# A two-block model on one core: keys, queries and attention of the sparse layer, rearranged

## What is computed

```python
# shared_kv, after the third FFN of the second block's first layer
kv = (u @ w_kv).reshape(b, s, 3, 2, N_KV_HEADS, HEAD_DIM)      # 3 branches, 2 key-value heads of 64
k_cmp = rms_norm(compress(kv[:, :, 0, 0], 0), kv_k_gain[0])    # 31 blocks of 32 tokens, stride 16
v_cmp = compress(kv[:, :, 0, 1], 1)                            # silu(flat @ phi_w1) @ phi_w2
k_slc = rope(rms_norm(kv[:, :, 1, 0], kv_k_gain[1]))           # and k_win in the same way
# nsa_mixer, after the next FFN: 16 query heads, 8 to a key-value head
q = rms_norm((u @ w_qg)[..., :1024].reshape(b, s, 16, 64), q_gain)
gates = sigmoid((u @ w_qg)[..., 1024:])                        # 48 columns
o = gates[0] * softmax(q @ k_cmp) @ v_cmp \
  + gates[1] * softmax(rope(q) @ k_slc) @ v_slc \
  + gates[2] * softmax(rope(q) @ k_win) @ v_win                # causal, no more than 512 keys
return o @ w_o
```

## Time and profile before

| | |
|---|---|
| median of 3 runs | 3986.0 us (3985.46 to 3986.86) |
| profiled execution, its own time | 3986.36 us |
| its span | 3984.6 us |
| TensorE busy, share of the span | 3708.1 us, 93% |
| VectorE busy | 1862.0 us, 47% |
| ScalarE busy | 1375.4 us, 35% |
| mean granted clock of TensorE | 0.955 |

### The profile page before, as it was taken

How to read it: one execution, slowest core, us unless ns; L and a number is a source line. 1 busy time by engine, 2 the same in 40 slices (tenths; PEclk the granted TensorE clock), 3 DMA queues, 4 the chain that set the end, 5 groups by cost and what they waited for, 6 DMA issues and landing times.

```text
span 3984.6 us, 49773 instructions
## 1 busy us (share of the span) xinstructions
PE 3708.1 (93%) x18908; PEld 2895.2 (73%) x18908; DVE 1862.0 (47%) x4004; ACT 1375.4 (35%) x2448; POOL 107.3 (3%) x183
## 2 busy tenths in 40 slices
PE   8879999989998999999999899999799997779999
PEld 3458966778887888777777678886688865557887
DVE  4656635566574333555445543331333327464333
ACT  1142212432233222555555542222222226463222
POOL 1100001011111000000000000000000000000000
PEclk9979999989999999999999999999699988999999
DMA  6500016336652222111111122321222210002222
GB/s 247 190 1 1 1 58 228 115 129 234 220 192 98 87 104 85 64 48 64 48 64 64 43 77 90 116 74 69 81 95 102 88 67 1 22 21 85 85 106 74
DMA packets 47289, 362.72 MB, mean 91 GB/s; under 512 B 5233, under 2 KB 5617, under 8 KB 28145
## 3 DMA queue, kind: packets, MB, share of 16 engines
q1 hardware_dynamic: 23616, 272.47, 18.7%
q0 software_dynamic: 23472, 87.50, 6.3%
HBM read 357.86 MB, written 2.10 MB: 90 GB/s over the span
## 4 chain that ended last, share of the span: by engine, by line
PE 81%; DVE 8%; issue 6%; ACT 2%; DVEq 1%; PEld 1%; DMA 0%; ACTq 0%; PEldq 0%; POOL 0%; SPq 0%; POOLq 0%
PE bank L792 19%; PE bank L798 19%; PE bank L797 19%; PE bank L755 6%; PE bank L1535 5%; PE bank L734 2%; PE bank L773 1%; PE bank L1869 1%; PE bank L1886 1%; PE bank L1857 1%; PE bank L708 1%; PE bank L722 1%; PE bank L1845 1%; DVE work_sb L2339 1%; DVE w_lo_sb L1154 1%
## 5 line engine op out<-in xcount | busy, mean ns | idle before, releaser
L792 PE MATMUL bank<-x_hi_sb,w_hi_sb 128*128 128x512 f32 x2592 | 1042.7, 402 | 62.5 <-DVE w_lo_sb L1154 15.5
L797 PE MATMUL bank<-x_lo_sb,w_hi_sb 128*128 128x512 f32 x2592 | 1019.6, 393 | 0.0
L798 PE MATMUL bank<-x_hi_sb,w_lo_sb 128*128 128x512 f32 x2592 | 1019.6, 393 | 0.0
L792 PEld LDWEIGHTS bank<-x_hi_sb,w_hi_sb 128*128 128x128 f32 x2592 | 493.1, 190 | 201.4 <-issue 77.5
L977 ACT ACTIVATE w_hi_sb<-slab_sb 128x1024 fp32r<-128x1024 f32 (+2 forms) x508 | 459.6, 930 | 403.2 <-PE bank L792 225.8
L1154 DVE TENSOR_TENSOR w_lo_sb<-slab_sb,w_hi_sb 128x1024 fp32r<-128x1024 f32 (+2 forms) x508 | 524.5, 1066 | 132.7 <-ACT w_hi_sb L977 116.2
L798 PEld LDWEIGHTS bank<-x_hi_sb,w_lo_sb 128*128 128x128 f32 x2592 | 493.0, 190 | 106.3
L797 PEld LDWEIGHTS bank<-x_lo_sb,w_hi_sb 128*128 128x128 f32 x2592 | 494.1, 191 | 96.3
L1305 DVE TENSOR_TENSOR hid_sb<-silu_gate_sb,bank 128x512 f32<-128x512 f32 x110 | 75.6, 688 | 624.2 <-PE bank L798 624.2
L792 PE MATMUL bank<-hid_hi_sb,w_hi_sb 128*128 128x512 f32 x880 | 343.3, 390 | 0.0
L798 PE MATMUL bank<-hid_hi_sb,w_lo_sb 128*128 128x512 f32 x880 | 342.8, 390 | 0.0
(11 more groups left out here) (336 smaller groups left out, 4095.2 us busy)
## 6 DMA issues: line engine op xcount, KB each, us to landing
slab_sb<-weights SPq DMA_DIRECT2D x81, 2048.0 KB, 7.7
slab_sb<-weights SPq DMA_DIRECT2D x44, 1536.0 KB, 6.4
keep_sb<-ada POOLq DMA_DIRECT2D x104, 512.0 KB, 4.8
slab_sb<-weights SPq DMA_DIRECT2D x20, 1280.0 KB, 5.9
work_sb<-ada POOLq DMA_DIRECT2D x49, 512.0 KB, 5.6
tables_sb<-ada POOLq DMA_DIRECT2D x7, 512.0 KB, 6.8
h_sb<-x SPq DMA_DIRECT2D x4, 512.0 KB, 7.4
out<-h_sb SPq DMA_DIRECT2D x8, 256.0 KB, 2.1
```

What stands on the lines that cost most here:

```text
L792: mm = pe.matmul(e.A.bank[s][:, :], w_hi[p][:, w], hi, start=first, stop=False)
L797: pe.matmul(e.A.bank[s][:, :], w_hi[p][:, w], lo, start=False, stop=False)
L798: return pe.matmul(e.A.bank[s][:, :], w_lo[p][:, w], hi, start=False, stop=last)
```

## The change

1. The weights of keys, compressed parts, values and all queries go the three-pass way. The key stage's order is: the 4 key tiles (an opening), the 2 compressed tiles, head sums, values, spread, compression of the keys, swap, compression of the values. The stages "kv" and "compress" are one.
2. The two query stages are one: tiles 0 to 3, 4, 5, head sums, 6, spread, 7, swap, gates, then head sums, spread and swap of tiles 4 to 7. The stream has both query slabs ahead of the gates. The squares are made per tile as a tile is copied out (act_head_tile). Since the engines come to the banks in different orders, lists of names (KV_USES, Q_USES) say which bank each use has.
3. Attention is written out once for 32 units and has no loop; the tiles come in pairs, one with its blocks of queries in rising and the other in falling order. q_now and its copies are gone, and so are the memsets ahead of the reductions. The gates' reciprocal is at DVE's first weighing.
4. ffn_2 and ffn_3 split three parts of the slab that follows them.

Helpers that are not shown stay as they are.

```diff
     *ffn_stream(3),
-    ("w_q_0", 1, 4096),
+    ("w_q", 2, 4096),
     ("gates", 1, 512),
-    ("w_q_1", 1, 4096),
     ("b_w_o", 2, 4096),
     *ffn_stream(4),
...
     w_kv = x["w_kv_2"].reshape(D, 3, 2, P)
-    w_kv = np.concatenate([w_kv[:, 0, 0], w_kv[:, 0, 1]] + twice(w_kv[:, 1, 0]) + twice(w_kv[:, 2, 0])
-                          + [w_kv[:, 1, 1], w_kv[:, 2, 1]], 1)
+    keys = slabs_by_tile(np.concatenate(twice(w_kv[:, 1, 0]) + twice(w_kv[:, 2, 0]), 1))
+    compressed = slabs_of(np.concatenate([w_kv[:, 0, 0], w_kv[:, 0, 1]], 1), P)
+    values = slabs_of(np.concatenate([w_kv[:, 1, 1], w_kv[:, 2, 1]], 1), 2 * P)
+    w_kv = np.concatenate([keys, np.concatenate([*compressed, *values], 1)[None]], 0)
...
+        def pe_tile_parts(e):
+            s = e.give(e.A, e.acc)
+            p = e.take(part, e.part)
+            for kt in range(KT):
+                mm = pe_product(e, s, p, slice(kt * P, (kt + 1) * P), x_hi[:, kt, :], x_lo[:, kt, :], kt == 0,
+                                kt == KT - 1)
+            mm.then_inc(e.A.full[s], 1)
+            e.owed = p
+        def pe_token_parts(e, parts, cols, stride, together=False):
+            pe = e.eng
+            per = KT // parts
+            seats = [e.give(e.A, e.acc)] * NB if together else [e.give(e.A, e.acc) for _ in range(NB)]
+            for i in range(parts):
+                p = e.take(part, e.part)
+                for b in range(NB):
+                    tokens = slice(b * P, (b + 1) * P)
+                    o = b * cols if together else 0
+                    out = bank[seats[b]][:, o:o + cols]
+                    for at in range(per):
+                        k, w = i * per + at, slice(at * stride, at * stride + cols)
+                        mm = pe.matmul(out, x_hi[:, k, tokens], w_hi[p][:, w], start=k == 0, stop=False)
+                        if e.owed is not None:
+                            mm.then_inc(part.free[e.owed], 1)
+                            e.owed = None
+                        pe.matmul(out, x_lo[:, k, tokens], w_hi[p][:, w], start=False, stop=False)
+                        mm = pe.matmul(out, x_hi[:, k, tokens], w_lo[p][:, w], start=False, stop=k == KT - 1)
+                    if i == parts - 1:
+                        if not together or b == NB - 1:
+                            mm.then_inc(e.A.full[seats[b]], 1)
+                    elif b == NB - 1:
+                        mm.then_inc(part.free[p], 1)
+            e.owed = p
+        def pe_head_cols(e, sqv, tiles):
+            pe = e.eng
+            s = e.give(e.A, e.acc)
+            for x in range(tiles):
+                pe.wait_ge(squared, e.nth(squared))
+                for b in range(NB):
+                    at = (x * NB + b) * 2
+                    mm = pe.matmul(bank[s][:, at:at + 2], sqv[:, x, b * P:(b + 1) * P], K("head2"), start=True, stop=True)
+            mm.then_inc(e.A.full[s], 1)
+        def act_head_tile(e, dst, square):
+            act = e.eng
+            s = e.take(e.A, e.acc)
+            act.activation(dst, bank[s][:, :], ACT.Copy)
+            act.activation(square, bank[s][:, :], ACT.Square).then_inc(squared, 1)
+            act.drain().then_inc(e.A.free[s], 1)
...
+        n_p = [cut(work, 12288, 2304), cut(work, 14592, 2304), xn.rearrange("p a b -> p (a b)")[:, 0:2304]]
+        n_pt = [cut(work, 0, 2304), sqf[:, 0:2304]]
...
+        KV_USES = ["k0", "k1", "k2", "k3", "c0", "c1", "cols", "v0", "v1", "v2", "v3", "spread0", "spread1", "spread2",
+                   "spread3", "swap0", "swap1", "swap2", "swap3", "second", "cmp_cols", "cmp_spread"]
+        Q_USES = ["q0", "q1", "q2", "q3", "q4", "q5", "cols0", "q6", "spread0", "spread1", "spread2", "spread3", "q7",
+                  "swap0", "swap1", "swap2", "swap3", "gates", "cols1", "spread4", "spread5", "spread6", "spread7",
+                  "swap4", "swap5", "swap6", "swap7"]
+        class Order:
+            def __init__(self, e, names):
+                self.seat, self.names, self.start = e.acc, names, e.acc.pos
+            def go(self, name):
+                self.seat.pos = self.start + self.names.index(name)
+        def sparse_units():
+            units = []
+            for g in range(0, KT, 2):
+                up = g % 4 == 0
+                for b in range(NB):
+                    units += [(g, b if up else NB - 1 - b), (g + 1, NB - 1 - b if up else b)]
+            return units
+        def attend_sparse(e, finish):
...
-            units = [(x, b) for x in range(2) for b in range(NB)]
+            units = sparse_units()
             n = len(units)
             heads = range(2)
+            opens = {next(i for i, u in enumerate(units) if u[0] == t) for t in range(KT)}
+            closes = {max(i for i, u in enumerate(units) if u[0] == t) for t in range(KT)}
+            outs = {}
...
-                        eng.matmul(e.S.bank[s][:, 0:keys], q_now[rows, pair if br == 0 else 2 + pair, q], k,
+                        eng.matmul(e.S.bank[s][:, 0:keys], (q_rot if br else q_raw)[rows, tile, q], k,
...
-                                eng.memset(small[:, 128 + 2 * br + hh:129 + 2 * br + hh], 0.0)
...
+                        if i == 1:
+                            eng.wait_ge(rooted, e.nth(rooted))
+                            e.link(eng.tensor_scalar(gates, gates, 1.0, None, ALU.add), dve_step)
+                            e.link(eng.reciprocal(gates, gates), dve_step)
...
-            pe_slab_opening(e, xn, normed)
-            pe_slab(e, range(2), KT, 512, lambda k: xn[:, k, :],
-                    more=[lambda sl: pe_token_major(e, sl, xn, KT, 256, 512, 256)])
-            pe_cols(e, sq, 4, NB, False, 2)
+            pe_parts_opening(e, x_hi, x_lo)
+            e.slab.next()
+            for _ in range(2):
+                pe_tile_parts(e)
+            pe_settle(e)
+            pe_head_cols(e, kv_sq, 4)
+            pe_token_parts(e, 2, 2 * P, 2 * P)
+            pe_settle(e)
+            pe.wait_ge(inverted, e.nth(inverted))
             for j in range(4):
                 pe_spread(e, NB, 2, j)
-            pe_swap(e, kv_raw, 4)
-            e.stage_end("kv")
...
+            pe.wait_ge(heads_ready, e.nth(heads_ready))
             pe_slab(e, (), 0, 0, None, more=[compress(0)])
+            pe_swap(e, kv_raw, 4)
             pe_slab(e, (), 0, 0, None, more=[compress(1)])
             for s in two:
-                pe.drain().then_inc(e.A.full[s], 1)
-            pe.wait_ge(hidden_ready, 1)
+                pe.drain().then_inc(e.S.full[s], 1)
+            pe.wait_ge(hidden_ready, 2)
...
-            for kv in range(2):
-                if kv == 0:
-                    pe_sums_close(e)
-                    pe_rms_spread(e)
-                    pe_slab_opening(e, xn, normed)
-                    pe_slab(e, (), KT, 64, None,
-                            more=[lambda sl: pe_token_major(e, sl, xn, KT, 0, 64, 48, together=True)])
-                else:
-                    pe_slab(e, range(4), KT, 512, lambda k: xn[:, k, :])
-                pe_cols(e, sq, 4, NB, False, 2)
-                for j in range(4):
-                    pe_spread(e, NB, 2, j)
-                pe_swap(e, q_raw, 4)
-                e.stage_end("sparse_q")
-                e.use(e.duo)
-                with repeat(pe, 2, e.rates(acc=2, sc=48, tp=28, weighed=8, copied=8, heads_ready=1)) as i:
-                    pe.wait_ge(heads_ready, e.nth(heads_ready))
-                    attend_sparse(e, kv, i, None)
-                e.use(e.single)
-                e.stage_end("sparse")
+            pe_sums_close(e)
+            pe_rms_spread(e)
+            pe_parts_opening(e, x_hi, x_lo)
+            e.slab.next()
+            pe_tile_parts(e)
+            pe_tile_parts(e)
+            pe_settle(e)
+            pe_head_cols(e, q_sq[:, 0:4, :], 4)
+            pe_tile_parts(e)
+            pe_settle(e)
+            pe.wait_ge(inverted, e.nth(inverted))
+            for j in range(4):
+                pe_spread(e, NB, 2, j)
+            pe_tile_parts(e)
+            pe_settle(e)
+            pe_swap(e, q_raw[:, 0:4, :], 4)
+            e.slab.next()
+            pe_token_parts(e, 1, 48, 64, together=True)
+            pe_settle(e)
+            pe_head_cols(e, q_sq[:, 4:8, :], 4)
+            pe.wait_ge(inverted, e.nth(inverted))
+            for j in range(4):
+                pe_spread(e, NB, 2, j)
+            pe_swap(e, q_raw[:, 4:8, :], 4)
+            e.stage_end("sparse_q")
+            e.use(e.duo)
+            attend_sparse(e, None)
+            e.use(e.single)
+            e.stage_end("sparse")
...
-            act_ffn(e, fold[:, 2, 1, :], h)
+            act_ffn(e, fold[:, 2, 1, :], h, (D, 3))
             e.stage_end("ffn_2")
+            e.slab.pos += 1
             act_sums_root(e)
-            act_shift(e, fold[:, 3, 1, :])
+            act_w_hi(e, 3, D)
+            act_split(e, fold[:, 3, 1, :])
+            order = Order(e, KV_USES)
+            for j in range(4):
```

(57 more changed lines are left out.)

151 lines of the change are left out of this document (63 added, 88 removed).

## The result

The changed kernel takes **3917.7 us** (median of 4 runs, 3915.52 to 3920.80) against 3985.7 us for the kernel before (median of 4, 3983.98 to 3986.86): a ratio of 0.983, 95% interval 0.9813 to 0.9847. That is 68 us faster. 51 were forecast, and the range of 3908 to 3954 holds it. The forecast's own spread, 3920 to 3950, does not: the result lies between it and rival A's 3900 to 3915. The profiled execution took 3920.8 us with a span of 3919.0; the one of before took 3986.4, so the two traces differ by 65.6 us, and this is what the stages have to add up to.

What follows compares the result with a forecast made beforehand. Chains of waits through keys with compression, queries and attention bound 474 us of a 3984.6 us span. Gains 19 + 15 + 20 = 54, less 3, take 3986.4 to 3935.4, forecast median 3935; range 3908 to 3954.

Steps and rivals of the forecast that it cites:

- rival A: Small products get cheap: clock up through compression (12 us), gates at low end (6), steps near 5.2 (16): 3900 to 3915; chance 0.16.
- Rival D: Key and query tails line up again behind an early wait, no attention gain: 3976 to 3986 us; chance 0.04.
- Rival C: TensorE's clock halves inside attention, 30 steps take 300 us instead of 172, kernel near 4063; chance 0.04.
- Rival B: Attention gives nothing, every step near 6.4 us; only keys and queries gain: 3950 to 3955; chance 0.10.
- Keys, 109.4 for 118.2: Key stage with compression, up to ffn_3's first product: 118.2 us instead of 137.25, 19 us gained.
- the compression, 25.8 in the sum: Key stage's 256 small matmuls: 27.8 us before, less 2 for coming from dense work.
- The values: Key stage's value products, three passes at half the stream each: 10.3 to 13.2 us, 12 taken.
- Queries, 108.3 for 105.2: The two query stages as one: 105.2 us instead of 120.0, 15 us gained.
- the gates, 11.5 taken: Query stage's 96 matmuls of 48 columns: 5 to 19 us, 11.5 taken near the two-pass row.
- Attention, 190.1 for 197: Attention in one piece, three of four fills and drains gone: 197 us instead of 217.0, 20 us gained.
- a step's length goes by the unit before it alone: Attention steps: 6.86 us after 512 keys, about 5.9 after 384, about 5.1 after 256 or 128; 5.74 per step.
- The 3 us taken off the sum: Taken off the 54 us gain, since the cold parts of two stages were set from the good side.

## Why the prediction was right, and where it was not

**Right:** faster, by the three stages named, each by its mechanism. The rotary tail went under the compression, the query tail under tiles 6 and 7 and the gates, three of four restarts went. Rival D (the overlap doesn't come) fell: ahead of the first two spreads stands a gap of 0.26 us, ahead of the last the 1 us that the sum had. Rival C fell: the clock is 0.99 from 3322 us on; it is at 0.50 only in the first 17 us. Rival B fell at 5.54 us a step. Part of rival A happened: the compression and the steps became cheap, the gates did not. That the time fell into the range is owed in part to this, since the range took rival A in; 3917.7 is 17 us below the forecast and outside its own spread.

**Keys, 109.4 for 118.2.** The failed term is the compression, 25.8 in the sum: it measured 18.2. The prediction took 2 us off "as PE comes to it from dense work"; the row it went by, PE busy and the clock at 0.50, shows what these matmuls do with a clock that is already down. It doesn't show what they do with one that is up. The run with the tail first settles that: same code, 27.1 us behind 7.75 us of idleness. Of the other terms, the swaps were 6.3 (6 taken), the spread 3.6 (5.3), the head sums 4.3 with their gap (5.3), the start 7.7 (9.0), the tail of 19.1 (19.4) as carried. The values were dearer, 14.7 for 12, and above the bounds of 10.3 to 13.2: behind the head sums and a gap of 0.6 us the clock was down (0.51 from 2769.5 to 2776), and the first 28 of 96 matmuls ran at 0.213 us. The rest ran at 0.120, inside the bounds of 0.107 to 0.137 a pass; those bounds allowed for no slow stretch.

**Queries, 108.3 for 105.2.** The failed term is the gates, 11.5 taken and 18.2 measured. The bounds were 5 and 19; the value was taken near a row whose clock was falling midway, but that row had 64 matmuls and this has 96, so more of them lie behind the fall. It belonged near the upper end. The rule of the Trainium skill (TensorE: Matmul & The Clock Gate, section on weight-path perf modes), that weights which are not fp32 and fill 128 columns load faster, gave nothing here: a gates matmul on fp32r weights takes 0.11 us at the upper level, and the fp32 head sums, whose weights are as large, 3.70/32 = 0.116. The same table of the skill gives that mode no gain for fp32, since it reads weights 32 bits at a time. The fp32r weights are as wide, so the prediction's 5 us stretched the rule, and no run here tests it on narrower ones. Tile 6 took 7.6 for 5.5, as it starts on the clock that the head sums had let fall (0.78). Cheaper were the start (7.6 for 9.0), the first head sums (3.6 for 4.9) and the first spread (3.6 for 5.3); tile 7 took 6.0 for 5.5, the swaps 3.1 for 3.7. What follows the gates came out as forecast, 22.9 for 24.4. That the stage is only 3 us off is luck: gates and tile 6 are 8.8 us above their terms, and start, head sums, spread, swaps and the end together some 6 below.

**Attention, 190.1 for 197.** 2.65 us to the first tick (4), 4.80 for the first step (4.5), 168.9 for 30 steps with the gate reciprocals among them (172.2 + 1.9), 13.7 of drain (14.4). The step that failed is the reading that a step's length goes by the unit before it alone. The classes were right for 512 keys (6.69, forecast 6.86) and roughly for 384 (5.57 to 6.08, forecast 5.9), but after 128 keys the mixed order has 3.80 to 4.77 where 5.1 was taken; after 256 it has 5.06 to 5.64, 0.25 more than taken on the mean. In rising order these classes (128, 256, 384, 512 keys) give 4.98, 5.42, 5.97 and 6.69. So a step depends on its other neighbours too. That the slack of a small unit is used where its scores and exponentials lie beside a large unit's transposes and copies is an argument; what the runs show of it is that the order loses most of its worth once the scores stand early.

**The clock rule.** The same page of the Trainium skill, section on the clock gate, says that activity releases the clock and idleness lowers it. The prediction held the trace of before against it. The runs say that both read one half: behind idleness it was down (0.50 behind the 7.75 us ahead of the compression), but in the kernel after it also fell with TensorE busy 7.60 of 7.6 us, while matmuls of 31 columns ran, and wide ones between them kept it at 1.00. So for these matmuls the rule is half of it: which matmuls keep TensorE busy matters, not only that it is busy. The prediction had both halves, but apart: rival A, at 0.16, had the clock still up from the dense work ahead, and its counter-argument had the gates' clock falling with PE busy. It had no case in which a stretch starts on the inherited level and loses it part way, which is what compression and gates both did.

The two errors of size, 9 us too dear for the keys and 7 for the attention, point the same way and the 3 us for the gates against them. The 3 us taken off the sum as a caution made it worse; without them 3932 would have stood.
